# Four of the last gather requests of a mixture-of-experts stage, each written as two requests of 120 and 8 partitions

## The reference

```python
def _peer(h, w_query, sub_keys, expert_u, expert_v):
    ...
        top, pos = lax.top_k(cand, PEER_TOPK)
        idx = jnp.take_along_axis(cidx, pos, axis=-1)
        g = jax.nn.softmax(top, axis=-1)
        act = jax.nn.gelu(jnp.einsum('mhkd,md->mhk', expert_u[idx], xb).astype(jnp.float32))
        w = (g * act).astype(xb.dtype)
        return jnp.einsum('mhk,mhkd->md', w, expert_v[idx])
```

## Time and profile before

| | |
|---|---|
| Median of three executions | 1339.31 us (1336.11 to 1339.74) |
| The profiled execution, its own time | 1336.45 us |
| Its span, first to last instruction | 1334.6 us |
| TensorE busy | 1181.7 us, 89% |
| VectorE busy | 869.0 us, 65% |
| GpSimd busy | 322.6 us, 24% |
| Gathers (q0) | 268.45 MB |
| First gather issued | 671.6 us |

### The profile page before, as it was taken

One profiled execution on the slowest core, in us unless ns is written; L12 is line 12 of the kernel. 1 busy time (PEld: TensorE's weight loads), 2 busy tenths in 40 slices (PEclk: granted clock), 3 DMA queues, 4 the chain that ended last, 5 costly groups with the idle time before them and its releaser, 6 DMA issues.

```text
span 1334.6 us, 14779 instructions
## 1 busy us (share of the span) xinstructions
PE 1181.7 (89%) x5152; PEld 709.0 (53%) x5152; DVE 869.0 (65%) x2323; ACT 315.8 (24%) x1016; POOL 322.6 (24%) x278
## 2 busy tenths in 40 slices
PE   8999899989999979998999889899878787787776
PEld 5876657867855757765566445445323233232232
DVE  2736845365542658685388678777777877777655
ACT  0114300243210233241132222223222222222222
POOL 0000000000000000000054444445654554454520
PEclk9999899999999999999999999999999899999999
DMA  8762045722344443534389999999999999999994
GB/s 342 288 244 87 41 189 197 305 102 75 115 190 152 159 170 134 216 142 171 127 330 425 425 423 426 424 424 424 423 423 423 423 424 424 422 423 423 424 423 196
DMA packets 50330, 386.91 MB, mean 290 GB/s; under 512 B 5712, under 2 KB 8400, under 8 KB 10832
## 3 DMA queue, kind: packets, MB, share of 16 engines
q0 software_dynamic: 36864, 268.45, 48.1%
q1 hardware_dynamic: 13392, 117.51, 23.4%
HBM read 384.89 MB, written 1.05 MB: 289 GB/s over the span
## 4 chain that ended last, share of the span: by engine, by line
PE 56%; DMA 32%; DVE 7%; ACT 3%; issue 2%; POOL 0%; SPq 0%; DVEq 0%; ACTq 0%
PE bank L523 22%; PE bank L529 14%; DMA hT<-peer_uv_in,arena 10%; DMA wring<-peer_uv_in,arena 9%; PE bank L1118 9%; DMA const<-peer_uv_in,arena 7%; DMA arena<-peer_uv_in,arena 6%; PE bank L564 2%; DVE arena L1573 2%; PE bank L597 1%; PE bank L754 1%; PE bank L667 1%; DVE arena L1581 1%; PE bank L920 1%; PE bank L726 1%
## 5 line engine op out<-in xcount | busy, mean ns | idle before, releaser
L1118 PE MATMUL bank<-arena 128*128 128x512 f32 x460 | 220.2, 615 | 45.8 <-ACT arena L1541 45.6
L1118 PE MATMUL bank<-wring,arena 128*128 128x512 f32 x340 | 162.2, 612 | 35.1 <-ACT arena L1541 35.1
L523 PE MATMUL bank<-wring,hT 128*128 128x256 f32 (+2 forms) x640 | 187.9, 451 | 5.9 <-ACT hT L1219 4.2
L529 PE MATMUL bank<-hT,wring 128*128 128x256 f32 (+1 forms) x1088 | 186.5, 331 | 0.2 <-ACT arena L1330 0.2
L529 PEld LDWEIGHTS bank<-hT,wring 128*128 128x128 f32 x1088 | 168.1, 191 | 24.2 <-issue 9.9
L2253 DVE CUSTOM_DVE_ANT_0 arena<-arena 128x1024 f32<-128x1024 f32 x115 | 140.6, 1224 | 58.9 <-DMA arena<-peer_uv_in,arena 57.4
L2348 POOL DMA_INDIRECT arena<-peer_uv_in,arena x115 | 138.1, 1201 | 160.3 <-PE bank L1118 126.3
L1118 PEld LDWEIGHTS bank<-arena 128*128 128x128 f32 x460 | 85.2, 195 | 163.4 <-issue 89.2
L2321 POOL TENSOR_TENSOR small<-small,const 128x1 f32<-128x1 f32 (+3 forms) x18 | 16.1, 896 | 634.6 <-DVEq L1585 288.9
L523 PEld LDWEIGHTS bank<-wring,hT 128*128 128x128 f32 x640 | 120.3, 191 | 66.2 <-issue 49.9
L2253 DVE CUSTOM_DVE_ANT_0 wring<-wring,arena 128x1024 f32<-128x1024 f32 x85 | 103.9, 1223 | 44.0 <-DMA wring<-peer_uv_in,arena 43.9
(11 more groups left out here) (210 smaller groups left out, 1288.0 us busy)
## 6 DMA issues: line engine op xcount, KB each, us to landing
wring<-w_in SPq DMA_DIRECT2D x22, 2048.0 KB, 8.4
wring<-ada_in SPq DMA_DIRECT2D x12, 2048.0 KB, 8.2
wring<-wo_in SPq DMA_DIRECT2D x5, 2048.0 KB, 8.7
wring<-cmp_in SPq DMA_DIRECT2D x2, 2048.0 KB, 8.0
wring<-br_in SPq DMA_DIRECT2D x2, 2048.0 KB, 8.5
arena<-pq_in SPq DMA_DIRECT2D x2, 2048.0 KB, 10.1
wring<-pq_in SPq DMA_DIRECT2D x2, 2048.0 KB, 8.6
wring<-w1b_in SPq DMA_DIRECT2D x2, 1120.0 KB, 7.9
```

What stands on the lines that cost most here:

```text
L523: ins = pe.matmul(bank[:, 0:cols], lhs[k], w[:, k, 0:cols], start=(k == 0), stop=(k == n - 1))
L529: ins = pe.matmul(bank[:, at:at + n_tok], w[:, k, col:col + P], rhs[:, k, :], start=(k == 0), stop=(k == KC - 1))
L1118: ins = pe.matmul(sums_of[half][:, :], diag[:, at % NDIAG, :], v_row[slot_of[at]][:, half * 512:(half + 1) * 512], start=(n == 0), stop=(n ...
```

## The change

Rows 226, 230, 234 and 238 (r = 2, 6, 10 and 14 of head 14) are gathered with two requests each: one for partitions 0 to 119 and one for partitions 120 to 127. The second reads its indices from a new small tile, `idx_tail`, in whose partitions 0 to 7 stands a copy of the indices of partitions 120 to 127 of head 14. SP makes this copy with a DMA from SBUF to SBUF of 8 partitions by 16 numbers, when `idx_ready` says that head 14's indices are there. POOL waits for it before each second request. Each half adds 16 to the buffer's semaphore, so the counts for which VectorE waits are worked out anew (`landed`). All else, the order of the rows and their buffers too, is as before.

```diff
+        idx_tail = take(TOPK).bitcast(I32)
...
+        SPLIT_HEAD = 14
+        SPLIT = [SPLIT_HEAD * TOPK + r for r in (2, 6, 10, 14)]
+        TAIL = 8
+        landed = [sum(2 if m in SPLIT else 1 for m in range(n + 1) if slot_of[m] == slot_of[n]) for n in range(ROWS)]
...
             for t in range(TT):
+                if t:
+                    sp.wait_ge(sem("idx_ready"), SPLIT_HEAD + 1)
+                    s = (SPLIT_HEAD % 2) * TOPK
+                    sp.dma_start(idx_tail[0:TAIL, :], idx[P - TAIL:P, s:s + TOPK]).then_inc(sem("idx_tail"), 16)
...
-                    dve.wait_ge(sem(f"row_full{slot_r}"), 16 * (use_no[at] + 1))
+                    dve.wait_ge(sem(f"row_full{slot_r}"), 16 * landed[at])
...
-                    pool.indirect_dma_start(out=pair[here], out_offset=None, in_=a["peer_uv"],
-                                            in_offset=bass.IndirectOffsetOnAxis(ap=idx[:, s:s + 1], axis=0)
+                    n = P - TAIL if at in SPLIT else P
+                    pool.indirect_dma_start(out=pair[here][0:n, :], out_offset=None, in_=a["peer_uv"],
+                                            in_offset=bass.IndirectOffsetOnAxis(ap=idx[0:n, s:s + 1], axis=0)
                                             ).then_inc(sem(f"row_full{here}"), 16)
+                    if at in SPLIT:
+                        pool.wait_ge(sem("idx_tail"), 16)
+                        pool.indirect_dma_start(out=pair[here][n:P, :], out_offset=None, in_=a["peer_uv"],
+                                                in_offset=bass.IndirectOffsetOnAxis(ap=idx_tail[0:TAIL, r:r + 1], axis=0)
+                                                ).then_inc(sem(f"row_full{here}"), 16)
```

## The result

The change is slower: the median of four executions is 1373.01 us (1368.45 to 1377.95) against 1339.14 us before (four executions, 1336.11 to 1339.74). The ratio is 1.025, with a 95% interval of 1.0225 to 1.0275, so 30 to 37 us are lost where I had forecast 6.3 us gained. The profiled execution took 1373.55 us, its span is 1371.7 us. TensorE is busy 1194.5 us, VectorE 869.8 us, GpSimd 335.3 us, with 282 instructions instead of 278.

A forecast was written before the change was run, and what follows sets the result against it. The DMA engines' gathers were taken as the bound, with one late engine at the end. Relieving it gave -6.3 us, copy and POOL 0: 1339.31 - 6.3 = 1333.0 us, range 1329.5 to 1341.0 us.

The forecast's parts named there:

- What bounds the kernel: In the gathers the DMA engines are always busy; at the end one late engine works alone, 7.6 us behind the next.
- the part on the requests: At the four split rows, 120 partitions go over fifteen engines and relieve the late one: 6.3 us less, 7.6 at best.
- eight others get 4 packets more, 1.24 us: Over the four split rows, the requests of 8 give eight engines 4 packets more each, 1.24 us.
- The left-out engine: At the split rows, the requests of 120 always skip one engine, the late one: 32 packets less, 9.9 us; chance 0.50.
- the first rival: At the split rows, the left-out engine changes from row to row: 1337.4 to 1339.9 us; chance 0.20.
- the second: At the split rows, the same engine is always left out, but not the late one: 1339.3 to 1340.6 us; chance 0.20.
- the instruction fetches of q8: Guess for the late engine at the end: 12 fetches all on it, 24 packets of 8 KB, 7.4 us.
- The slow one: At the split rows, 120 partitions go over eight engines: 1348.0 us with the late engine among them; chance 0.08.
- GpSimd and the wait for the copy: Ahead of the split rows, four more issues, 3.8 to 8.2 us, stay hidden and POOL does not wait: 0 us.
- the copy and its bytes: SP's copy ahead of row 226 lands between 1209.5 and 1217 us, its 64-byte pieces negligible: price 0.

The follow-up runs named there:

- 120 alone: The change with its four requests of 8 left out, so partitions 120 to 127 of those rows are not gathered: 1370.27 us, ratio 1.021 to the kernel before.
- the probes: Two kernels with extra gathers of various partition counts issued ahead of row 0, one step waited for before the next: 1377.98 and 1395.30 us, one execution each.
- the copy alone: The change with no row split, its index tile, SP's copy and POOL's wait kept: 1346.48 us, ratio 1.0036 to the kernel before.
- one split: The change with only row 226 split, the other three rows whole: 1355.34 us, ratio 1.0122 to the kernel before.
- four, neighbours: The change with rows 226, 227, 228 and 229 split in place of its own four: 1369.01 us, ratio 1.0217 to the kernel before.
- four, head 2: The change with rows 34, 38, 42 and 46 of head 2 split and none of head 14: 1369.56 us, ratio 1.0191 to the kernel before.
- four, 112 and 16: The change with its four rows split as 112 and 16 partitions, not 120 and 8: 1364.53 us, ratio 1.02 to the kernel before.

## Why the prediction was wrong

**What bounds the kernel:** right, and more so than I drew from it. The gathers' rate sets the end, each us lost there is lost in the whole, and a late engine holds the last rows. Both held in the changed kernel, and from the last landing to the end it was 9.2 us as before.

**The step that failed** stands in the part on the requests: "eight others get 4 packets more, 1.24 us; the rest are as before". All terms of the sum counted packets and priced each at the 0.309 us of the earlier trace rows. That price is one of full requests. In a request of 120 a packet takes 0.56 us alone, and beside others, in 1250 to 1255 us of the changed kernel, the packets of all engines take 0.53 us or more, 0.65 us on average. So a term was missing, the rate at which a request with another shape moves, and it was 27.1 us in the changed kernel. I had written that no row of before shows a request of fewer than 128 partitions, and had drawn from it that the *sharing* was unknown; the *duration* was just as unknown, and the range had to hold it. No row of before gives that term a size. An assumed doubling of a packet's time over the 12 us in which the engines pass a request would be 6 us for each of the four, 24 us: a bound from above that leans on no measurement, but of the right size.

**The left-out engine** (-9.9 us for the late one): wrong. The late engine was not the one left out in any of the four requests of 120. In the trace of the change its increments, the last of each row, stand 7.6 us or more behind those of all the others at rows 224 to 239. At the split rows its increment for the 120 comes 4.8, 4.9, 5.5 and 4.6 us behind that of the row before, the time of eight slow packets; an engine that got none would add next to nothing. The chain shows it for rows 229 and 230 (the second is split), where VectorE waits for the late engine:

```profile
1281.92 1.24 DVE arena L2262 x2
...
1287.08 1.23 DVE arena L2262 x2
```

It is the same with the 120 alone (5.1, 5.0, 4.9 and 4.6 us) and in the other kernels that split rows of head 14, and at the end the late engine is still about 8 us behind the next. By the rule of the Trainium skill (DMA: Bandwidth & Descriptors, Why a DMA increments its semaphore by 16 and not by 1) fifteen engines take 120 partitions, eight take 8 and four take 124; the probes agree in all three (15 to 16 packets under way at a time for the 120, at most eight for the 8, four for the 124). It also says that the fifteen begin somewhere else each time. That is the first rival; the second, the same engine each time and not the late one, fits the increments as well, and no run here names an engine, so which of the two it is stays open. The prediction also guessed at what makes that engine late, the instruction fetches of q8. The trace of before points to q14 (instruction): from row 146 on the engine needs 3.4 us for a row instead of 2.5 at rows 166, 188, 208 and 231 alone, and each of these lands 2.0 to 3.3 us behind the start of an 8 KB packet of q14. Two other packets of q14 in that time have no such step, so this is likely and not shown.

**The rivals:** the first two had the late engine right and the time wrong, as they too priced packets at 0.309 us. The slow one gave 1348.0 us at most, and its eight engines for 120 partitions are not what the probe shows. None of my cases reached 1373 us.

**GpSimd and the wait for the copy** (0 us): right; no wait, and four more issues of 0.90 to 1.34 us while the DMA engines had work in line throughout.

**The tile's place:** I priced the copy and its bytes and not the 64 bytes by which the tile moves its neighbours. They cost 5.1 us (3 to 7) by themselves. The three gather buffers that began at a multiple of 256 bytes no longer do.

**The sum from the traces:** 75 us at 268 GB/s cost 27.1 us, and 568 us at 0.5 to 0.7% less rate cost 3 to 4 us, together 30 to 31 of the 32.2 us between first issue and last dot product.

| | slow stretch costs | late engine behind the next at the end | first issue to last dot product, more than with the copy alone (656.9 us) | ratio to before |
|---|---|---|---|---|
| one split | 5.9 us | 9.6 us | 8.2 us | 1.0122 |
| four, neighbours | 17.7 us | 10.0 us | 21.8 us | 1.0217 |
| four, head 2 | 20.5 us | 10.7 us | 25.7 us | 1.0191 |
| four, 112 and 16 | 19.1 us | 9.1 us | 20.8 us | 1.02 |
| four, 120 alone | 25.2 us | 7.7 us | 28.5 us | 1.021 |
| four, the change | 27.1 us | 8.1 us | 29.1 us | 1.025 |

The third column is a second cost. In the seven traces without a split row the late engine ends 6.2 to 8.2 us behind the next (7.2 with the copy alone), in four of the six here 9.1 to 10.7 us; the window for the four neighbours shows it alone for over 10 us:

```profile
1343.00:1353.40 10.40, 7.92 (x19) 3.16 (x18) 6.37 (x17) 2.60 (x10) 0.00 (x0) 1.00 0.06 27
```

The slow stretch and what the late engine loses beyond 7.2 us add up to the fourth column within 3 us. With the 5.1 us of the moved tile on top, the sum lies within the interval of the whole in all six.

**Still open** is why engines slow each other down in such a request. The Trainium skill (DMA: Bandwidth & Descriptors, The descriptor swizzle) says that in a full request each engine writes partitions that reach SBUF through a port of its own, {0 to 3, 32 to 35} for the first. A request dealt out by neighbouring partitions would break that. That is my inference. The 0.56 us of the 120 fit, and the half of the 124's packets at 0.32 us fit in part; but the 16 partitions, which would be four engines to a port, should then be slower than they are. No run tells which port an engine uses.

## What to carry to other kernels

Where a kernel is bound by gathers, leave them at 128 partitions: a request of 120, 112 or 64 moved at 201 to 224 GB/s where the full one moved at 311 alone, and in a stream the full ones beside it were slow too. When a change issues a request of a new shape, its rate is an unknown as large as its bytes; measure one alone before counting packets. And watch that no small tile moves the buffers behind it: here 64 bytes took three gather buffers off a multiple of 256 bytes and cost 5 us.

## What was unexpected of the hardware

- A gather packet of 8 KB took 309 ns in nearly every case when all buffers began at a multiple of 256 bytes, and 309 to 324 ns when fifteen of eighteen did not; 427 against 424 GB/s, and 421 with none of the eighteen there. The Trainium skill (DMA: Bandwidth & Descriptors, How a descriptor splits into AXI transactions) says that a descriptor which does not start at a multiple of 256 bytes begins its first transaction at the boundary below, and that the bytes before the start still cost time; the direction agrees, though the page speaks of what a transaction reads and here it is the written side that is off.
- The DMA share stayed at 1.02 while the rate fell from 420 to 268 GB/s. The share tells that engines hold packets, not how fast the bytes move.
- 124 partitions had four packets under way at a time and made 388 small packets, and took 17.2 us from issue to landing where 128 took 5.4 us.
